# Projection panels moved among the head-norm spreads and ahead of the differential heads, modulation groups and bias copies placed anew, and GpSimd's products taking two tensors

## Chip, cores and metric

The kernel runs on one core of a Trainium2 chip. The metric is the device time of one execution in microseconds, lower is better.

## The reference

Two networks run one after the other, in float32. Block 1 (two layers, 256 tokens and 16 meta tokens, width 1024) does in each layer: an RMS norm; one input projection `h @ w_in` that gives the queries, keys and values of three attentions and 3 x 1024 gate logits; latent attention (8 heads, RMS-normed and rotated q and k); stick-breaking attention (8 heads, a suffix sum of log weights in place of the softmax); differential attention (4 heads, `softmax(q1 k1) - lam * softmax(q2 k2)`, its output normed again); `merged = sum over three branches of sigmoid(gate) * (out @ w_branch)`; an output projection; and a feed-forward with squared ReLU and width 4096. The last layer computes 256 tokens only after the attentions' keys.

Block 2 (two layers, 256 tokens and 256 context tokens) has a SwiGLU of width 2816, a mixer (retention in layer 0, neighbourhood attention in layer 1) and another SwiGLU. Each is entered through a norm with scale and shift and left through a gate. These come from the modulation, which depends on no token:

```
s_c, s_cc = silu(c), silu(c_ctx)
ml, mc = s_c @ w_mod[i] + b_mod[i], s_cc @ w_mod[i] + b_mod[i]     # 9 * 1024 columns each, for i in 0, 1
```

## The kernel before

**Weights.** All large weights come as 632 panels of 128 x 1024 floats. SyncE loads a panel into one of four slots of `raw` as soon as TensorE has finished the panel that was there (L354). ScalarE copies it rounded to float32r (`whi`, L961), VectorE subtracts to get the rest (`wlo`, L1487), and TensorE multiplies three times: high weights by high inputs, high by low, low by high (L454 to L456 for features, L544 to L546 for the token-major values). One panel of features is 24 multiplications; four quarter panels (`token_quarter`) make 512 value columns and hold three PSUM banks until the last. Panels are used strictly in the order in which the host lays them out.

**Order of work.** It is written out by hand, once per engine; the engines meet through semaphore counts, so a step that moves on TensorE must move in ScalarE's and VectorE's programs too. Four PSUM banks (0 to 3) go round for results of panels, banks 4 to 7 serve attention. In each layer of block 1 TensorE does: eight feature panels; the latent up-projections with one panel after each of four of them (`UP_FILL`); `units`, 24 heads of queries and keys, each a sum of squares (L657) and a rotation (L660), with a filler panel after two of every three (`UNIT_FILL`, 14 of 16; fillers 0 to 7 are features, 8 to 15 quarter panels), then the last two fillers (L667) while ScalarE takes roots and VectorE their reciprocal (L1721); `spread`, which brings the inverse roots of each head to all partitions (L676), VectorE rescaling the head right behind it (`normed`, L1729), at most four spreads ahead of it; latent heads, stick heads 0 to 7, differential heads 0 to 3 with 2, 2, 2 and 1 features (`DIFF_FILL`, L815); the branch panels, for each pair `mp` of output chunks and branch `br` in turn; then the output projection and the feed-forward. Branch panels with `br` 2 need `olo`, the low part of the normed differential outputs.

**Gates and exps.** ScalarE evacuates a gate feature with `gate()` (which first waits for its panel) and computes the exps of the next differential head with `diff_exps`, in program order.

**Modulation.** The 144 chunks of 128 outputs of both layers are made in 36 groups of four on GpSimd, beside everything else (L370 to L420). A group works through four panels of `w_mod` with 16 products (a weight panel by one column of `cs`, L384) and 14 sums (L386), strictly in turn, into `macc`, which exists once. Then `mod_group` on TensorE (L474) sums `macc` over the partitions with eight matmuls (L480, recorded as sixteen), after a wait for all of the group's steps, and GpSimd's next group waits for that:

```
pool.wait_ge(mod_done, g)                  # before the first product of group g
...
lane.take(mod_step, MS)                    # TensorE: 30 steps of the group are done
```

The constants in L82 to L84 say after which unit, stick head, differential head, tile or residual chunk TensorE takes a group. Each layer of block 1 has nine: units, end of the spreads, a stick head, a differential head, after branch pair 1, before the feed-forward, after 20 of its tiles, and after chunks m=1 and m=5 of its second product (`residual_tiles`, K=32, four panels for each m). The rest stand in block 2: after 12, 24 and 36 tiles of a SwiGLU's first product, after m=1 and m=5 of its second, and in the retention likewise.

Between group 12 (the one taken in layer 1's differential heads) and group 13 (the one taken at its branch panels) GpSimd issues sixteen copies that write the attention bias table, repeated for every column, to DRAM (L427).

Of the kernel before, what the change touches and what calls it, by code (L numbers as in the profile page):

```python
# [81 lines left out]
MOD_UNIT, MOD_STICK, MOD_DIFF, MOD_BRANCH = (12,), (2,), (1,), (1,)  # L82
MOD_FF, MOD_FF2, MOD_RET, MOD_FF3 = (1, 5), (1, 5), (1, 5), (1,)
# [5 lines left out]
UNIT_FILL = tuple(u for u in range(21) if u % 3)  # L89
UNIT_LAG = 2  # L90
DIFF_FILL = (2, 2, 2, 1)
# [89 lines left out]
def build_program(nc, t):  # L181

    ctx = ExitStack()
    with ctx:
# [181 lines left out]
        def _(pool):  # L366
# [7 lines left out]
            def mod_group(g, last=False):  # L374
# [3 lines left out]
                def step(out, a, b, op):  # L378

                    nonlocal steps  # L380
                    if steps or not (isinstance(g, int) and g == 0):
                        pool.wait_ge(mod_step, g * MS + steps)
                    if op is ALU.mult:
                        pool.tensor_scalar(out, a, b, None, op).then_inc(mod_step, 1)  # L384
                    else:
                        pool.tensor_tensor(out, a, b, op).then_inc(mod_step, 1)  # L386
                    steps += 1

                acc = [macc[:, s * 512:(s + 1) * 512] for s in range(2)]
                for q in range(4):  # L390
                    s = q % 2
                    w = [modraw[:, s * PW + k * 512:s * PW + (k + 1) * 512] for k in range(2)]
                    c = [[cs[:, 4 * q + 2 * k + stream:4 * q + 2 * k + stream + 1] for k in range(2)] for stream in range(2)]
# [54 lines left out]
        def _(pe):  # L448
# [189 lines left out]
            def units():  # L638
# [28 lines left out]
                for n in range(len(UNIT_FILL), 16):  # L667
                    filler(n)
                lane.settle(u_rot)
                lane.take(u_inv)  # L670

# [41 lines left out]
            for layer in range(DEPTH):  # L713
# [10 lines left out]
                units()  # L724

                for j in range(2 * MH):
# [3 lines left out]
                    spread(j, 4 + j % 4)  # L730
                lane.settle(u_out)
                scores(4, qm, km, 0, 0, MQK)
                scores(5, qm, km, T1, 0, MQK)
                for j in range(2 * MH, 24):
                    lane.take(u_out, lag=2)
                    spread(j, 6 + j % 2)
                mod_group()
# [70 lines left out]
                lane.take(arg_ready)  # L808

                for hh in range(DH):  # L810
# [9 lines left out]
                    if hh in MOD_DIFF:  # L820
                        mod_group()
# [21 lines left out]
                lane.take(olo_ready, DH)  # L843
                branch(0, 2)
                for mp in range(1, NC // 2):
                    for br in range(3):
                        branch(mp, br)
                    if mp in MOD_BRANCH:
                        mod_group()
# [102 lines left out]
        def _(act):  # L952
# [98 lines left out]
            for layer in range(DEPTH):  # L1051
# [88 lines left out]
                for n in range(len(UNIT_FILL), 16):  # L1140
                    filler(n)
                lane.tile.add()
# [27 lines left out]
                exps(0, 0)  # L1170
                for hh in range(MH):
# [45 lines left out]
                head_hi(4 + (SH - 1) // 2, 64 * ((SH - 1) % 2))  # L1217

                for hh in range(DH):
# [11 lines left out]
                    lane.tile.add(1 + (hh in MOD_DIFF))  # L1231
# [21 lines left out]
                for mp in range(NC // 2):  # L1253
                    for br in range(3):
                        next_panel()
                        lane.tile.add(2)
                        if br == 0 and mp + 1 < NC // 2:
                            sigmoids(mp + 1)
# [213 lines left out]
        def _(dve):  # L1472
# [169 lines left out]
            for layer in range(DEPTH):  # L1642
# [180 lines left out]
                head_lo(4 + (SH - 1) // 2, 64 * ((SH - 1) % 2))  # L1823

# [4 lines left out]
                for hh in range(DH):  # L1829
# [19 lines left out]
                    if hh - 1 in MOD_DIFF:  # L1849
                        mod_tiles()  # L1850
# [21 lines left out]
                def branch(mp, br):  # L1872
# [23 lines left out]
                    elif mp:  # L1896
# [8 lines left out]
                branch(0, 1)  # L1905
                branch(0, 2)
                for mp in range(1, NC // 2):
                    for br in range(3):
                        branch(mp, br)
                    if mp in MOD_BRANCH:  # L1910
# [344 lines left out]
def all_panels(a):  # L2255

    out = []
    for l in range(DEPTH):
# [9 lines left out]
        out.append(wb.transpose(3, 0, 2, 4, 1, 5).reshape(-1, P, PW))  # L2268
# [79 lines left out]
```

## Time and profile before

| What | Value |
|---|---|
| median of 3 runs | 3621.97 us (3619.17 to 3635.52) |
| the profiled execution | 3621.35 us |
| span of its instructions | 3619.6 us |
| TensorE busy, share of the span | 3306.0 us, 91% |
| VectorE, ScalarE, GpSimd busy | 50%, 36%, 53% |
| mean granted TensorE clock | 0.944 |
| panels, mean traffic | 632 of 512 KB, 119 GB/s |

Times in rows are microseconds from the start of the span, unless marked ns. PE is TensorE's matmul, PEld its weight load, DVE VectorE, ACT ScalarE, POOL GpSimd, SP SyncE. PEclk is the granted share of TensorE's clock of 2.4 GHz, so 0.5 is 1.2 GHz. "Idle before <- X" is the engine's idle time just before the instruction and what ended it. A float32 matmul is recorded as two instructions, so the sixteen of L480 are eight in the code. Matmul ends are modelled and overlap the next start.

### The profile page before, as it was taken

How to read it: one execution, taken by the hardware profiler on the slowest of the kernel's cores; microseconds unless marked ns; L12 is line 12 of the kernel's file. 1: busy time of each engine (PE TensorE's matmuls, PEld its weight loads, DVE VectorE, ACT ScalarE, POOL GpSimd, SP SyncE). 2: the span in 40 equal slices, each digit the busy share in tenths (PEclk: the TensorE clock that was granted, in tenths of full speed). 3: DMA queues.
4: the chain of work that ended last, by engine and by line, in shares of the span. 5: the costliest groups of instructions: out<-in, count | busy, mean ns of one | idle time of the engine just before them, and what ended most of it. 6: DMA issues, size and time to landing. Idle time of an engine off the chain costs nothing.

```text
span 3619.6 us, 49159 instructions
## 1 busy us (share of the span) xinstructions
PE 3306.0 (91%) x18070; PEld 2752.1 (76%) x18070; DVE 1805.0 (50%) x2502; ACT 1292.0 (36%) x2179; POOL 1908.0 (53%) x1277
## 2 busy tenths in 40 slices
PE   7999789899984898899999889989999999998899
PEld 5676689876763898788877757768887888785799
DVE  5665666456543674544352344354435443426554
ACT  3445445343542363322232233232223222235443
POOL 6565878925665788378655003846876565001000
PEclk9989889998987899999999999999999999999999
DMA  4322345532265465233333102323333333331254
GB/s 174 111 82 82 128 146 198 183 124 92 94 122 110 142 212 181 100 122 127 120 119 115 64 0 93 116 99 116 128 122 105 110 122 105 101 111 54 83 184 158
DMA packets 120281, 430.37 MB, mean 119 GB/s; under 512 B 13856, under 2 KB 17184, under 8 KB 119728
## 3 DMA queue, kind: packets, MB, share of 16 engines
q1 hardware_dynamic: 93632, 335.24, 27.5%
q0 software_dynamic: 24576, 86.46, 7.9%
q10 hardware_dynamic: 1904, 6.36, 0.5%
q8 instruction: 113, 1.85, 0.2%
q14 instruction: 56, 0.46, 0.0%
HBM read 426.95 MB, written 8.85 MB: 120 GB/s over the span
## 4 chain that ended last, share of the span: by engine, by line
PE 56%; DVE 5%; POOL 3%; issue 1%; ACT 1%; DMA 0%; DVEq 0%; ACTq 0%; SPq 0%; POOLq 0%
PE ps L454 16%; PE ps L456 15%; PE ps L455 15%; DVE xlo L1542 1%; PE ps L544 1%; PE ps L545 1%; PE ps L546 1%; PE ps L480 1%; POOL macc L386 1%; PE ps L927 1%; DVE tmp L1548 1%; PE ps L882 1%; POOL modraw L384 1%; POOL mprod L384 1%; PE ps L871 1%
## 5 line engine op out<-in xcount | busy, mean ns | idle before, releaser
L1487 DVE TENSOR_TENSOR wlo<-raw,whi 128x1024 fp32r<-128x1024 f32 x632 | 877.7, 1390 | 1087.6 <-ACT whi L961 1064.7
L961 ACT ACTIVATE whi<-raw 128x1024 fp32r<-128x1024 f32 x632 | 668.1, 1058 | 1525.9 <-PE ps L456 1083.9
L454 PE MATMUL ps<-xhi,whi 128*128 128x512 f32 (+2 forms) x3008 | 1033.1, 343 | 48.3 <-DVE xlo L1542 33.1
L456 PE MATMUL ps<-xhi,wlo 128*128 128x512 f32 (+2 forms) x3008 | 1015.5, 338 | 0.0
L455 PE MATMUL ps<-xlo,whi 128*128 128x512 f32 (+2 forms) x3008 | 1015.3, 338 | 0.0
L454 PEld LDWEIGHTS ps<-xhi,whi 128*128 128x128 f32 x3008 | 581.6, 193 | 130.6 <-issue 44.4
L456 PEld LDWEIGHTS ps<-xhi,wlo 128*128 128x128 f32 x3008 | 581.0, 193 | 55.1
L455 PEld LDWEIGHTS ps<-xlo,whi 128*128 128x128 f32 x3008 | 581.9, 193 | 53.9
L384 POOL TENSOR_SCALAR macc<-modraw,cs 128x512 f32<-128x512 f32 x36 | 74.6, 2072 | 949.6 <-PE ps L480 939.0
L384 POOL TENSOR_SCALAR modraw<-modraw,cs 128x512 f32<-128x512 f32 x288 | 526.8, 1829 | 27.6
L384 POOL TENSOR_SCALAR mprod<-modraw,cs 128x512 f32<-128x512 f32 x252 | 447.3, 1775 | 18.9 <-POOL macc L386 0.2
L386 POOL TENSOR_TENSOR macc<-macc,mprod 128x512 f32<-128x512 f32 x252 | 361.4, 1434 | 21.0
L386 POOL TENSOR_TENSOR macc<-macc,modraw 128x512 f32<-128x512 f32 x216 | 327.1, 1514 | 17.5
L454 PE MATMUL ps<-ghi,whi 128*128 128x512 f32 (+1 forms) x704 | 259.0, 368 | 0.0
L455 PE MATMUL ps<-glo,whi 128*128 128x512 f32 (+1 forms) x704 | 258.2, 367 | 0.0
L456 PE MATMUL ps<-ghi,wlo 128*128 128x512 f32 (+1 forms) x704 | 258.2, 367 | 0.0
L443 POOL DMA_DIRECT2D bia<-bias_by_column x32 | 20.9, 658 | 309.0 <-DVE nsc L2141 189.9
L480 PE MATMUL ps<-con,macc 128*128 128x1 f32 x576 | 83.3, 274 | 79.3 <-POOL macc L386 79.3
L456 PEld LDWEIGHTS ps<-ghi,wlo 128*128 128x128 f32 x704 | 132.3, 188 | 24.0
L455 PEld LDWEIGHTS ps<-glo,whi 128*128 128x128 f32 x704 | 132.4, 188 | 23.6
L454 PEld LDWEIGHTS ps<-ghi,whi 128*128 128x128 f32 x704 | 132.4, 188 | 23.6
L454 PE MATMUL ps<-fhi,whi 128*128 128x272 f32 (+1 forms) x512 | 148.3, 290 | 1.5 <-issue 1.5
(339 smaller groups left out, 4782.3 us busy)
## 6 DMA issues: line engine op xcount, KB each, us to landing
raw<-in_panels SPq DMA_DIRECT2D x632, 512.0 KB, 3.3
modraw<-in_mod POOLq DMA_DIRECT2D x144, 512.0 KB, 3.8
bias_by_column<-in_rpb POOLq DMA_DIRECT2D x16, 476.2 KB, 38.4
bia<-bias_by_column POOLq DMA_DIRECT2D x32, 96.0 KB, 2.6
rtab<-in_rtab ACTq DMA_DIRECT2D x2, 1312.0 KB, 9.4
wuq<-in_wuq ACTq DMA_DIRECT2D x2, 768.0 KB, 6.6
con<-in_con SPq DMA_DIRECT2D x1, 1345.5 KB, 12.2
h<-in_x SPq DMA_DIRECT2D x1, 1088.0 KB, 6.8
```

The source lines that it names most:

```text
L384: pool.tensor_scalar(out, a, b, None, op).then_inc(mod_step, 1)
L386: pool.tensor_tensor(out, a, b, op).then_inc(mod_step, 1)
L454: pe.matmul(out, w_hi, x_hi, start=start, stop=False)
L455: pe.matmul(out, w_hi, x_lo, start=False, stop=False)
L456: return pe.matmul(out, w_lo, x_hi, start=False, stop=stop)
L480: last = pe.matmul(bank(b, 2 * j + s, 2 * j + s + 1), macc[:, s * 512 + j * P:s * 512 + (j + 1) * P], ones[:, 0:1], start=True, stop=True)
L544: pe.matmul(out, xh, wh(4 * kk, 512), start=(k == 0), stop=False)
L545: pe.matmul(out, xl, wh(4 * kk, 512), start=False, stop=False)
L546: last = pe.matmul(out, xh, wl(4 * kk, 512), start=False, stop=(k == NC - 1))
L871: last = pe.matmul(bank(4 + i // 2, (i % 2) * 256, (i % 2) * 256 + 256), qk2[:, k + kt * P:k + (kt + 1) * P], qk2[:, q + q0:q + q0 + NX], ...
L961: act.activation(whi[:, s * PW:(s + 1) * PW], raw[:, s * PW:(s + 1) * PW], ACT.Copy).then_inc(hi_split, 1)
L1487: dve.tensor_tensor(wlo[:, s * PW:(s + 1) * PW], raw[:, s * PW:(s + 1) * PW], whi[:, s * PW:(s + 1) * PW].bitcast(F32), ALU.subtract).then ...
```

## The change

Five things change; the arithmetic of the result is the same.

1. GpSimd's products are `tensor_tensor` with the column of `cs` broadcast along 512 elements by a stride of zero. Before they were `tensor_scalar` with the column as a per-partition scalar.
2. Groups are taken after unit 6 in place of 12, after stick heads 0 and 6 in place of stick head 2 and differential head 1, and after m=6 in place of m=5 of the second products. The order of groups against the bias copies stays, so the group ahead of the copies is now the one of stick head 6.
3. The unit loop has a filler after every other unit (11), one filler follows it, and one each stands after spreads 4, 9, 14 and 19.
4. Two features stand ahead of the differential heads, whose own number falls from 2, 2, 2, 1 to 1, 2, 1, 1.
5. Branch panel (1, 0) comes ahead of (0, 2), and the low part of a merged pair is made one panel later.

```diff
-MOD_UNIT, MOD_STICK, MOD_DIFF, MOD_BRANCH = (12,), (2,), (1,), (1,)
-MOD_FF, MOD_FF2, MOD_RET, MOD_FF3 = (1, 5), (1, 5), (1, 5), (1,)
+MOD_UNIT, MOD_STICK, MOD_BRANCH = (6,), (0, 6), (1,)
+MOD_FF, MOD_FF2, MOD_RET, MOD_FF3 = (1, 6), (1, 6), (1, 6), (1,)
-UNIT_FILL = tuple(u for u in range(21) if u % 3)
+UNIT_FILL = tuple(u for u in range(1, 22) if u % 2)
+UNIT_FILLS, SPREAD_FILL = len(UNIT_FILL) + 1, (4, 9, 14, 19)
-DIFF_FILL = (2, 2, 2, 1)
+BRANCH_ORDER = ((0, 0), (0, 1), (1, 0), (0, 2), (1, 1), (1, 2)) + tuple((mp, br) for mp in (2, 3) for br in range(3))
+DIFF_LEAD, DIFF_FILL = 2, (1, 2, 1, 1)
...
 # gpsimd
-                    if op is ALU.mult:
-                        pool.tensor_scalar(out, a, b, None, op).then_inc(mod_step, 1)
-                    else:
-                        pool.tensor_tensor(out, a, b, op).then_inc(mod_step, 1)
+                    pool.tensor_tensor(out, a, b, op).then_inc(mod_step, 1)
...
-                    c = [[cs[:, 4 * q + 2 * k + stream:4 * q + 2 * k + stream + 1] for k in range(2)] for stream in range(2)]
+                    c = [[cs[:, 4 * q + 2 * k + stream:4 * q + 2 * k + stream + 1].broadcast_to([P, 512]) for k in range(2)] for stream in range(2)]
...
 # tensor
-                for n in range(len(UNIT_FILL), 16):
+                for n in range(len(UNIT_FILL), UNIT_FILLS):
                     filler(n)
...
                     spread(j, 4 + j % 4)
+                    if j in SPREAD_FILL:
+                        filler(UNIT_FILLS + SPREAD_FILL.index(j))
...
                 lane.take(arg_ready)
+                for _ in range(DIFF_LEAD):
+                    feature(T)
...
-                lane.take(olo_ready, DH)
-                branch(0, 2)
-                for mp in range(1, NC // 2):
-                    for br in range(3):
-                        branch(mp, br)
-                    if mp in MOD_BRANCH:
+                for mp, br in BRANCH_ORDER[2:]:
+                    if (mp, br) == (0, 2):
+                        lane.take(olo_ready, DH)
+                    branch(mp, br)
+                    if br == 2 and mp in MOD_BRANCH:
                         mod_group()
...
 # scalar
-                for n in range(len(UNIT_FILL), 16):
+                for n in range(len(UNIT_FILL), 15):
                     filler(n)
-                lane.tile.add()
...
                 exps(0, 0)
+                filler(15)
+                lane.tile.add()
...
                 head_hi(4 + (SH - 1) // 2, 64 * ((SH - 1) % 2))
+                lane.tile.add(SH - 1 in MOD_STICK)
+                for _ in range(DIFF_LEAD):
+                    gate()
...
 # vector
                 for j in range(2 * MH):
                     normed(j)
+                    if j == 3:
+                        for n in range(len(UNIT_FILL), UNIT_FILLS):
+                            filler(n)
+                    elif j > 4 and j - 5 in SPREAD_FILL:
+                        filler(UNIT_FILLS + SPREAD_FILL.index(j - 5))
...
                 for j in range(2 * MH + 4, 24):
                     normed(j)
+                    if j == 20:
+                        filler(14)
                 latent_probs(0)
-                for n in range(len(UNIT_FILL), 16):
-                    filler(n)
+                filler(15)
...
-                    for _ in range(DIFF_FILL[hh - 1] if hh else 1):
+                    for _ in range(DIFF_FILL[hh - 1] if hh else 1 + DIFF_LEAD):
...
-                    elif mp:
+                    if br == 1 and mp:
                         merged_lo(mp - 1)
...
 # host
-        out.append(wb.transpose(3, 0, 2, 4, 1, 5).reshape(-1, P, PW))
+        out.append(wb.transpose(3, 0, 2, 4, 1, 5).reshape(-1, P, PW)[[3 * mp + br for mp, br in BRANCH_ORDER]])
```

## Rows read from the trace of the kernel before

**Rows 1.** TensorE's list of waits: who ended them, us in total, times, longest

```profile
PE ps L480 <- POOL macc L386: 79.3, 6, 33.4
...
PE ps L454 <- DVE xlo L1542: 33.1, 25, 3.3
...
PE ps L454 <- DVE olo L1904: 6.3, 2, 3.1
```

**Rows 2.** timeline, TensorE, L480: start us, us, instruction, count, [idle before]

```profile
425.48 3.54 PE L480 MATMUL ps<-con,macc 128*128 128x1 f32 x16 [16.44 <-POOL macc L386]
...
627.66 1.84 PE L480 MATMUL ps<-con,macc 128*128 128x1 f32 x16
...
688.62 3.54 PE L480 MATMUL ps<-con,macc 128*128 128x1 f32 x16 [10.77 <-POOL macc L386]
...
1175.83 3.54 PE L480 MATMUL ps<-con,macc 128*128 128x1 f32 x16 [33.42 <-POOL macc L386]
...
1427.75 3.54 PE L480 MATMUL ps<-con,macc 128*128 128x1 f32 x16 [11.36 <-POOL macc L386]
...
2343.57 3.54 PE L480 MATMUL ps<-con,macc 128*128 128x1 f32 x16 [7.14 <-POOL macc L386]
```

**Rows 3.** timeline, GpSimd, L427: the sixteen bias copies

```profile
1042.45 11.86 POOL L427 DMA_DIRECT2D bias_by_column<-in_rpb  x15
...
1121.00 0.79 POOL L427 DMA_DIRECT2D bias_by_column<-in_rpb  x1 [66.69 <-issue]
```

**Rows 4.** windows: stretch, length, busy us per engine, PEclk, DMA share, GB/s

```profile
88.00:168.00 80.00, 79.63 (x411) 53.61 (x412) 46.02 (x80) 37.01 (x73) 35.51 (x23) 1.00 0.32 106
177.00:215.00 38.00, 37.16 (x139) 24.63 (x138) 20.63 (x56) 6.88 (x23) 16.86 (x13) 0.55 0.09 31
337.00:352.00 15.00, 11.38 (x50) 9.39 (x51) 9.05 (x29) 3.42 (x15) 8.84 (x7) 0.66 0.16 54
425.00:433.00 8.00, 7.52 (x34) 7.55 (x35) 0.17 (x1) 0.00 (x0) 4.63 (x5) 0.51 0.21 66
989.00:996.00 7.00, 7.00 (x24) 4.09 (x24) 2.60 (x6) 2.11 (x5) 6.63 (x5) 0.52 0.01 2
```

**Rows 5.** page, part 5: GpSimd's products (L384) and one kind of sum

```profile
L384 POOL TENSOR_SCALAR macc<-modraw,cs 128x512 f32<-128x512 f32 x36 | 74.6, 2072 | 949.6 <-PE ps L480 939.0
...
L384 POOL TENSOR_SCALAR mprod<-modraw,cs 128x512 f32<-128x512 f32 x252 | 447.3, 1775 | 18.9 <-POOL macc L386 0.2
...
L386 POOL TENSOR_TENSOR macc<-macc,mprod 128x512 f32<-128x512 f32 x252 | 361.4, 1434 | 21.0
```

**Rows 6.** lines L384 and L386: ns min/median/max, first and last start

```profile
L384 POOL TENSOR_SCALAR mprod<-modraw,cs x252: 1564/1575/3473, 14.8 to 3024.6; 128x512 f32<-128x512 f32 x126
...
L386 POOL TENSOR_TENSOR macc<-macc,modraw x216: 1261/1302/2882, 34.9 to 3033.3; 128x512 f32<-128x512 f32 x108
```

**Rows 7.** timeline, TensorE: last products of stick heads 0 and 6, both layers

```profile
273.22 0.38 PE L805 MATMUL ps<-stick_z,vs 128*64 128x128 f32 x2
...
326.50 0.38 PE L805 MATMUL ps<-stick_z,vs 128*64 128x128 f32 x2
...
969.34 0.38 PE L805 MATMUL ps<-stick_z,vs 128*64 128x128 f32 x2
...
1024.57 0.38 PE L805 MATMUL ps<-stick_z,vs 128*64 128x128 f32 x2
```

**Rows 8.** DMA issues between 1040 and 1125 us: KB each, median us to landing

```profile
raw<-in_panels SPq DMA_DIRECT2D x8, 512.0 KB, 20.9
```

**Rows 9.** timeline, TensorE: first of two quarter panels; the first sixteen spreads

```profile
168.80 0.50 PE L544 MATMUL ps<-whi,xhi 128*128 128x512 f32 x1
...
177.34 11.96 PE L676 MATMUL ps<-rs,con 32*96 32x272 f32 x32
```

**Rows 10.** timeline, DVE: the reciprocal of the head norms' roots

```profile
174.73 1.84 DVE L1721 RECIPROCAL rs<-rs 32x272 f32<-32x272 f32 x1
```

**Rows 11.** timeline, TensorE: transposes of differential head 0, layer 0

```profile
340.62 1.35 PE L692 MATMUL ps<-con,att 128*128 128x128 f32 x6 [4.27 <-DVE att L1844]
```

More of the change, by code:

```diff
@@ L88 @@
 UP_FILL = (3, 7, 11, 15)
-UNIT_FILL = tuple(u for u in range(21) if u % 3)
+UNIT_FILL = tuple(u for u in range(1, 22) if u % 2)
+UNIT_FILLS, SPREAD_FILL = len(UNIT_FILL) + 1, (4, 9, 14, 19)
+assert UNIT_FILLS + len(SPREAD_FILL) == 16
 UNIT_LAG = 2
-DIFF_FILL = (2, 2, 2, 1)
+BRANCH_ORDER = ((0, 0), (0, 1), (1, 0), (0, 2), (1, 1), (1, 2)) + tuple((mp, br) for mp in (2, 3) for br in range(3))
+DIFF_LEAD, DIFF_FILL = 2, (1, 2, 1, 1)
 GATE_ORDER = tuple(range(2 * NC, 3 * NC)) + tuple(range(2 * NC))
@@ L670, in units @@
                 lane.take(u_inv)
+                return filler
             def spread(j, b):
@@ L723, in _ @@
                 up()
-                units()
+                filler = units()
                 for j in range(2 * MH):
@@ L736, in _ @@
                     spread(j, 6 + j % 2)
+                    if j in SPREAD_FILL:
+                        filler(UNIT_FILLS + SPREAD_FILL.index(j))
                 mod_group()
@@ L819, in _ @@
                     values(new_bank(), vd, hh * P, P, 0, 1728)
-                    if hh in MOD_DIFF:
-                        mod_group()
                 lane.take(sc_used, 2)
@@ L1230, in _ @@
                     act.activation(dout[:, hh * T1:(hh + 1) * T1], bank(b, 0, T1), ACT.Copy).then_inc(bank_free[b], 1)
-                    lane.tile.add(1 + (hh in MOD_DIFF))
+                    lane.tile.add()
                 lane.take(do_ps)
@@ L1251, in _ @@
                     act.activation(ohi[:, c * T1:(c + 1) * T1], dout[:, hh * T1:(hh + 1) * T1], ACT.Copy).then_inc(ohi_ready, 1)
[L1253 to L1258, printed above, removed]
+                for mp, br in BRANCH_ORDER:
+                    next_panel()
+                    lane.tile.add(2)
+                    if br == 0 and mp + 1 < NC // 2:
+                        sigmoids(mp + 1)
+                    if br < 2:
+                        continue
                     lane.tile.add(mp in MOD_BRANCH)
@@ L1823, in _ @@
                 head_lo(4 + (SH - 1) // 2, 64 * ((SH - 1) % 2))
+                if SH - 1 in MOD_STICK:
+                    mod_tiles()
+                lane.tile.add(DIFF_LEAD)
                 lam_init = 0.8 - 0.6 * math.exp(-0.3 * layer)
@@ L1845, in _ @@
                     last.then_inc(p_ready, 1)
-                    for _ in range(DIFF_FILL[hh - 1] if hh else 1):
+                    for _ in range(DIFF_FILL[hh - 1] if hh else 1 + DIFF_LEAD):
                         lane.panel.add()
                         split()
-                    if hh - 1 in MOD_DIFF:
-                        mod_tiles()
                     lane.tile.add(DIFF_FILL[hh] + 1)
@@ L1904, in _ @@
                     dve.tensor_tensor(olo[:, c * T1:(c + 1) * T1], v, ohi[:, c * T1:(c + 1) * T1].bitcast(F32), ALU.subtract).then_inc(olo_ready, 1)
[L1905 to L1910, printed above, removed]
+                for mp, br in BRANCH_ORDER[1:]:
+                    branch(mp, br)
+                    if br == 2 and mp in MOD_BRANCH:
                         mod_tiles()
```

## The prediction

> **What bounds the kernel now.** I read TensorE's (PE's) list of waits, the timeline at each long wait, what GpSimd (POOL) did before it, and the granted clock by stage. PE is the busiest engine and ends nearly every stage, so time comes only from its stalls and from stretches at half its clock. The largest stall is for modulation: 79.3 us in six waits of L480 for POOL's last sum [rows 1], five of them real: 16.4, 10.8, 33.4, 11.4 and 7.1 us [rows 2]. One POOL group lasts 54.0 us: it starts behind the sixteenth bias copy at 1121.8 and PE gets it at 1175.8 [rows 2, 3]. The 33.4 us is not arithmetic alone: POOL issues fifteen copies at 1042.5, stands 66.7 us, and only then begins the group that PE wants at 1142.4 [rows 3]. The other loss is clock. From 177 to 215 us, where the inverse roots are spread, the granted clock is 0.55 (1.2 GHz most of the time) though PE is counted busy 37.2 of 38 us; around the first differential head it is 0.66, and after the 16.4 us wait 0.51 [rows 4].
>
> **Groups moved, products changed.** A group is 16 products and 14 sums. Products as TENSOR_SCALAR take 1775 ns on average, sums of two tensors 1434 ns [rows 5]. No row has a product with a broadcast second tensor. Bounds: 1.26 us, the shortest two-tensor instruction, and 2.88, the longest [rows 6]; I take 1.47, since size and number of streams are those of the sums. A group gets 16 x 0.3 = 4.8 us shorter: 49.2.
>
> The rows show products at 1575 ns and sums at 1302 ns at the median, the two-tensor form being the quicker [rows 6]. The Trainium skill (GPSIMD Engine Reference, Elementwise — side-by-side cycle accounting) says the opposite: two inputs share one read port, 2.6 cycles an element against 1.8 in the best one-input loop. By that page a product would gain 0.34 us (an estimate from its figures) and the sum below would come out above 3550; the trace's order is against it.
>
> Wait by wait:
> - Layer 0, branch panels, 16.4 us. The group before it leaves the differential heads for stick head 6, over at 326.9 [rows 7]. POOL starts near 329 and ends by 378 (383 at the old price); PE asks at 409.0 [rows 2]. Gone. Its feeder, from stick head 0 (273.6) to 6: 53.3 us less 2 for PE's own modulation products leaves 51 [rows 7], 2 more than 49.2. Late next if the price doesn't fall: 54 against 51.
> - Second feed-forward product of layer 0, m=5 to m=6, 10.8 us. From m=1 (627.7) PE reached m=5 at 677.85 [rows 2], so 12.1 us per m with the group's 1.84 taken off; it will ask at 690, and even the old POOL was ready at 688.5. Gone.
> - The same in layer 1 (256 columns for 272, so 11.4 per m), 11.4 us: PE asks when the old POOL was ready. In the retention residual (2 panels of 512 columns per m, again about 11.4), 7.1 us. Both gone.
> - After a wait PE ran some 7.5 us at half clock (8 us at 0.51 [rows 4]), 3.6 us lost. Four waits gone give 14.5.
> - Layer 1, branch panels, 33.4 us: the group ahead of the bias copies now starts after stick head 0 (969.7, plus 2) and ends at about 1021; the copies start 21 us earlier than at 1042.5. They took 78.6 us [rows 3]; more panels beside them may add 0 to 4, I take 2. The next group ends at 1021.4 + 80.6 + 49.2, about 1151.5, for 1175.8: gain 24 (14 to 31, with products at 1.8 or 1.3). PE gets there sooner than before: in this stretch panels need 20.9 us to land [rows 8] and starve the differential heads, while a stick head uses one panel in 8 to 9 us and hides that. What PE gains there becomes wait for POOL, so nothing else in layer 1 between stick head 6 and the branches counts.
>
> Sum: 16.4 + 10.8 + 11.4 + 7.1 + 24 + 14.5 = 84.2.
>
> **Panels among the spreads.** Two quarter panels took 8.5 us ahead of the spreads (168.8 to 177.3) [rows 9]; one stays there, four now stand after spreads 4, 9, 14 and 19, three come out of the unit loop. PE's work is unchanged. In the unit loop DVE is busy 46 of 80 us at full clock [rows 4], so with thinner filling PE stays the bound. The gain is clock: 0.55 over 38 us [rows 4] is 17 us lost in layer 0, and about 15 in layer 1, which repeats it. Against it: the cover of the root chain shrinks. The last reciprocal starts at 174.7, takes 1.84 and ends 0.8 us before PE needs it [rows 9, 10]; one quarter (4.3 us) less cover and one weight split less ahead of it on DVE leave PE a wait of 1 to 2 us, and a short fall of the clock may remain. I take 13.5 + 12 = 25.5 (8 to 31). ACT's and DVE's splits for these panels stand among the rescalings, which may lag four spreads; a quarter panel of PE work covers them, and without that cover each would cost PE the time of a split.
>
> **Lead of the differential heads.** PE waits 4.27 us for head 0 [rows 11], then runs at 0.66 over 15 us [rows 4]: about 9 us. Two features (6 us, from 12.1 for four panels) ahead of it cover DVE's scaling. But the exps of head 1 now queue on ACT behind two gates, some 7 us later, and the copies of head 0's transposes behind them; heads 0, 2 and 3 have one feature as cover. I keep 7.5 in layer 0 (3 to 9); layer 1's is inside its POOL wait. The branch order puts (1,0) ahead of the wait for olo, 3.1 us in each layer [rows 1]: 3.1 in layer 0, layer 1's hidden likewise. The merged low parts come one panel later, far ahead of their use: nothing.
>
> **Costs.** A group between two stick heads leaves a stretch without a panel; in layer 1 that after head 2 fell to 0.54 for 7 us [rows 4], in layer 0 it didn't. Three such places count now (0 and 6, and 0 in layer 1) for two: -4.5, nearer to the bad case since the scores behind head 6 are longer (+3.5 to -7). POOL reads two streams all the time, and DVE's two-input work feels it; PE waits 33.1 us for the low parts of normed inputs [rows 1], and an eighth more is -4 (0 to -10).
>
> Net: 84.2 + 25.5 + 7.5 + 3.1 - 4.5 - 4 = 111.8. The profiled execution took 3621.35 us (span 3619.6, 1.75 around it), 0.6 below the median of the three runs. 3621.35 - 111.8 = 3509.6; I say 3510.
>
> **Rivals.**
> - The broadcast product costs what the scalar one did. For: the same loop may bind both. It loses 9.6 in layer 1's chain, 3 at stick head 6 and 1.7 of clock: 3524.
> - The products get slower, to the 2072 ns that the first of each group takes [rows 5]: two reads through one port, beside DVE. A group of 58.8. Waits: 7.8 at stick head 6, 19.2 in layer 1 (two groups), 2.3 and 2.3 in the residuals, 10 of clock: 3552. Against it, every sum reads two streams and has a median of 1302 ns. It is the direction that the GPSIMD page of the Trainium skill gives.
> - Slower than before: the stride-zero operand costs a second pass, 2 x 1.43 = 2.9 us, a group of 72. PE then waits at stick head 6 (21), layer 0's m=6 (12), layer 1's branches (2 x 23) and m=6 (15.5), retention (15.5), and at the groups 62 and 61 us apart in the first feed-forward product (20 panels) and from there to m=1 (12 panels and two m), 10 and 11 in each layer, 42; with 14 of clock, 3510 + 166 = 3676. It decides from a product of about 2.6 us, where such waits make up the 112. Only single disturbed sums are that long.
> - The spreads gain nothing: the roots' wait grows, DVE's splits hold up the rescaling, the clock falls again. For: this stretch has the thinnest PE work; against: units with panels between them run at 1.00 [rows 4]. 3535.
> - That the change doesn't do what it says is unlikely: order and weights move together.
>
> **Chances.** Forecast 0.60; price unchanged 0.12; spreads without gain 0.14; slower products 0.08; second pass 0.05; the rest 0.01. A difference of 0.5% (18 us) is about what a measurement of this kernel can tell from none. Faster 0.91, same 0.04, slower 0.05. The forecast's own terms vary together by some 20 (spreads 17 down, 5 up; copies 10 and 7). With 3524, 3535 and 3552 inside, the range is 3486 to 3553.
>
> **What would show it.** Right: L384 as TENSOR_TENSOR near 1.5 us, groups near 49; one wait of PE for POOL, about 35 us, at layer 1's branches; a granted clock near 1.0 from 165 to 205; no 4.27 us gap at head 0. Wrong: products of 1.8 or more, L480 waits at stick head 6, a clock near 0.5 among the spreads, PE waiting over 3 us for the reciprocal.

## The result, and the profile after

The changed kernel took 3591.03 us at the median (3589.59 to 3595.97), the kernel before 3621.97 (3615.06 to 3635.52), five runs each: a ratio of 0.9911, 95% interval 0.9887 to 0.9935. The gain is 31 us, not 112, and 3591 lies 38 us above the top of the range. The runs of before that were shared with the experiments had medians of 3621 to 3627 us in each batch, so the experiments are compared by their ratios as well as by their medians. One of e3's four runs took 8115.93 us and counts as slow, so e3's ratio and its median below are of the other three.

The page of the changed kernel, its span and busy time by engine:

```profile
span 3594.2 us, 49156 instructions
PE 3309.6 (92%) x18070; PEld 2750.5 (77%) x18070; DVE 1987.9 (55%) x2502; ACT 1296.0 (36%) x2179; POOL 1646.8 (46%) x1277
```

The same view of before had DVE at 1805.0 and POOL at 1908.0 us. GpSimd is busy for 261 us less. VectorE is busy for 183 us more, though nothing was given to it. GpSimd's groups of instructions, which answer to [rows 5]:

```profile
L386 POOL TENSOR_TENSOR macc<-macc,mprod 128x512 f32<-128x512 f32 x252 | 388.5, 1542 | 19.8
L386 POOL TENSOR_TENSOR macc<-macc,modraw 128x512 f32<-128x512 f32 x216 | 344.5, 1595 | 16.9
L386 POOL TENSOR_TENSOR mprod<-modraw,cs 128x512 f32<-128x512 f32 x252 | 321.3, 1275 | 13.8
L386 POOL TENSOR_TENSOR macc<-modraw,cs 128x512 f32<-128x512 f32 x36 | 46.8, 1299 | 1187.4 <-PE ps L480 1176.6 <-ACT cs L1046 10.8
```

The products (`mprod`) fell from 1775 ns on average [rows 5] to 1275, below the 1470 I took. The sums rose from 1434 to 1542. TensorE's list of waits, of the changed kernel, against [rows 1] (us in total, times, longest):

```profile
PE ps L454 <- DVE xlo L1551: 47.5, 29, 5.2
PE ps L705 <- ACT att L1231: 31.9, 2, 16.5
PE ps L573 <- DVE sq L1535: 25.7, 14, 8.5
...
PE ps L454 <- DVE wlo L1496: 10.9, 18, 2.6
```

The 79.3 us for GpSimd are gone from the top of the list. What is left of the largest one, 33.4 us [rows 2], is 1.56 us, and the bias copies run from 1006.0 to 1087.1, 81 us, where I had said 80.6 [rows 3]. Timelines of the changed kernel, TensorE and GpSimd:

```profile
1132.20 1.92 PE L480 MATMUL ps<-con,macc 128*128 128x1 f32 x16 [1.56 <-POOL macc L386]
```

```profile
1006.04 11.95 POOL L427 DMA_DIRECT2D bias_by_column<-in_rpb  x15
1086.32 0.80 POOL L427 DMA_DIRECT2D bias_by_column<-in_rpb  x1 [68.33 <-issue]
```

So nearly 78 us of waits for GpSimd went and the kernel gained 31. Longer waits stand for VectorE's low parts: xlo from 33.1 to 47.5 us, the weights' low parts (wlo) from 3.6 us in 2 waits to 10.9 in 18. The second line of the list, 31.9 us in which TensorE stands for ScalarE's copies of the transposes (`att`) in layer 1's differential heads, has two lines of before as its counterpart, 26.6 us together:

```profile
PE ps L704 <- ACT att L1223: 15.1, 1, 15.1
PE ps L704 <- ACT att L1224: 11.5, 1, 11.5
```

The time between stages (read off the timeline by each stage's first matrix product) shows where it was lost, in us:

```
stretch                               before  after   e1     e3
layer 0, head norms to spreads         88.3   78.5   73.3   71.7
layer 0, spreads to stick heads        87.9   97.7   97.4   97.5
layer 0, stick heads to diff. output  117.9  119.9  131.5  115.7
layer 0, to the next norm             112.7   95.5   89.4   79.3
layer 0, feed-forward                 226.8  221.4  213.3  213.8
layer 1, stick heads to diff. output  151.9  153.7  152.7  134.6
layer 1, to the next norm             131.0  103.3  108.2   78.5
swiglu behind layer 1                 390.3  397.2  392.5  384.4
```

The first two rows belong together, since four quarter panels moved from the one to the other: 176.2 us before and 176.2 after. (e1 and e3 are experiments below.)

### The profile page after: what moved, and what is told of

Same layout as the page of the kernel before. It is cut to its first block, busy times and chain, and to the rows that moved or that the text cites. A ratio compares the mean times of both kernels' runs of the same rounds, so it can differ in the third digit from the quotient of the medians.

```text
span 3594.2 us, 49156 instructions
## 1 busy us (share of the span) xinstructions
PE 3309.6 (92%) x18070; PEld 2750.5 (77%) x18070; DVE 1987.9 (55%) x2502; ACT 1296.0 (36%) x2179; POOL 1646.8 (46%) x1277
## 4 chain that ended last, share of the span: by engine, by line
PE 58%; DVE 6%; issue 2%; ACT 1%; DMA 1%; DVEq 0%; ACTq 0%; SPq 0%
PE ps L454 16%; PE ps L455 16%; PE ps L456 16%; DVE xlo L1551 2%; PE ps L544 1%; PE ps L546 1%; PE ps L545 1%; PE ps L480 1%; PE ps L931 1%; DVE tmp L1557 1%; PE ps L886 1%; DVE wlo L1496 1%; DMA raw<-in_panels 1%; PE ps L875 1%; PE ps L902 1%
## 5 line engine op out<-in xcount | busy, mean ns | idle before, releaser
L1496 DVE TENSOR_TENSOR wlo<-raw,whi 128x1024 fp32r<-128x1024 f32 x632 | 942.5, 1492 | 1006.0 <-ACT whi L965 977.3
L454 PE MATMUL ps<-xhi,whi 128*128 128x512 f32 (+2 forms) x3008 | 1041.9, 346 | 69.4 <-DVE xlo L1551 47.5
L386 POOL TENSOR_TENSOR macc<-modraw,cs 128x512 f32<-128x512 f32 x36 | 46.8, 1299 | 1187.4 <-PE ps L480 1176.6
L386 POOL TENSOR_TENSOR macc<-macc,mprod 128x512 f32<-128x512 f32 x252 | 388.5, 1542 | 19.8
L386 POOL TENSOR_TENSOR modraw<-modraw,cs 128x512 f32<-128x512 f32 x288 | 369.8, 1284 | 22.6
L386 POOL TENSOR_TENSOR macc<-macc,modraw 128x512 f32<-128x512 f32 x216 | 344.5, 1595 | 16.9
L386 POOL TENSOR_TENSOR mprod<-modraw,cs 128x512 f32<-128x512 f32 x252 | 321.3, 1275 | 13.8
L443 POOL DMA_DIRECT2D bia<-bias_by_column x32 | 20.9, 657 | 317.4 <-DVE nsc L2154 189.9
L1983 DVE TENSOR_TENSOR sq<-tmp,ps 128x512 f32<-128x512 f32 (+1 forms) x88 | 54.6, 621 | 172.8 <-PE ps L456 172.0
```

Source lines behind the costliest of these rows:

```text
L454: pe.matmul(out, w_hi, x_hi, start=start, stop=False)
L1496: dve.tensor_tensor(wlo[:, s * PW:(s + 1) * PW], raw[:, s * PW:(s + 1) * PW], whi[:, s * PW:(s + 1) * PW].bitcast(F32), ALU.subtract).then ...
L1983: dve.tensor_tensor(w_, v, bank(b, 0, T), ALU.mult).then_inc(bank_free[b], 1)
```

## The experiments

**Theory A:** products with two streams hold up VectorE's operations that read two tensors from SBUF, and that takes back what the rest gains. **Rivals:** the shorter products are good and something else was lost (the panels' new places, a collision of transfers), or the products are harmless and the groups simply lay better before.

### The products' form, alone and taken back

e1 is the changed kernel with scalar products (and the coefficient not broadcast, which the lines below leave out). e2 is the kernel before with the same lines the other way, so that it has products of two tensors. The edit of e1:

```diff
-                    pool.tensor_tensor(out, a, b, op).then_inc(mod_step, 1)
+                    if op is ALU.mult:
+                        pool.tensor_scalar(out, a, b, None, op).then_inc(mod_step, 1)
+                    else:
+                        pool.tensor_tensor(out, a, b, op).then_inc(mod_step, 1)
```

> The changed kernel with GpSimd's products as before (TENSOR_SCALAR); order, groups and panels stay changed. Theory A (the missing gain went to VectorE: products that read two streams block its two-input work, which then holds TensorE): wlo falls from 1492 to under 1400 ns, VectorE's busy time by 100 us or more, a block 2 SwiGLU beside modulation from 397 and 399 to 390 and 391 us; back come some 20 us at layer 1's branches and 3 to 5 at stick head 6 in each layer; together 3545 to 3575 us, below the changed kernel's 3591. Rival B (the missing gain lies in the moved panels and groups themselves): no such gain, and the waits for GpSimd return: 3600 to 3615 us.

> The kernel before with the products alone changed to two tensors. Theory A: groups of about 47 us, four of the five long waits gone and layer 1's down to some 25 us, worth 65 us with the clock behind them, but VectorE slowed by 150 us or more and TensorE held in norms and feed-forward: 3600 to 3625 us, no clear gain. Rival B: the whole 65 us show: 3550 to 3565 us.

Measured: 3556.21 us for e1 (ratio 0.9809, 0.9788 to 0.9830) and 3620.78 for e2 (0.9990, 0.9976 to 1.0004), each in the band of theory A. Taking the new products out of the change makes it 35 us faster; put alone into before they gain nothing, though TensorE's waits for GpSimd fall there from 79.3 to 32.3 us. VectorE's busy time goes with the form both times, on the page of e1 and of e2:

```profile
PE 3302.0 (93%) x18070; PEld 2748.1 (77%) x18070; DVE 1804.9 (51%) x2502; ACT 1293.5 (36%) x2179; POOL 1905.6 (54%) x1277
```

```profile
PE 3332.1 (92%) x18070; PEld 2768.0 (76%) x18070; DVE 1954.3 (54%) x2502; ACT 1293.0 (36%) x2179; POOL 1646.1 (45%) x1277
```

### How much GpSimd does, and what it reads

e3 narrows every operation of GpSimd from 512 to 64 columns (it leaves out seven eighths of the modulation). e4 reads a dense 512-column tensor of constants in place of the broadcast coefficient (its modulation is another one). The lines that matter, without e3's clearing of `macc` and e4's wait for the constants at the start:

```diff
-                    pool.tensor_tensor(out, a, b, op).then_inc(mod_step, 1)
+                    pool.tensor_tensor(out[:, 0:64], a[:, 0:64], b[:, 0:64], op).then_inc(mod_step, 1)
```

```diff
-                    c = [[cs[:, 4 * q + 2 * k + stream:4 * q + 2 * k + stream + 1].broadcast_to([P, 512]) for k in range(2)] for stream in range(2)]
+                    c = [[con[:, 128 * k + 64 * stream:128 * k + 64 * stream + 512] for k in range(2)] for stream in range(2)]
```

> The changed kernel with every product and sum of the modulation over 64 of 512 columns, so the modulation of block 2 is left out for the rest; GpSimd is nearly idle, its DMAs, steps and waits stay. Theory A: no contention and no wait for GpSimd: wlo at 1230 to 1260 ns, 3525 to 3550 us. Rival B: TensorE never waited for more than 2 us for GpSimd in the changed kernel, so 3580 to 3592 us.

> The changed kernel with a 512-wide tile of the constants as the products' second tensor in place of the column repeated by a stride of zero; the modulation is computed with wrong factors. Does the repeated column cost less, for GpSimd or for VectorE? Theory A1 (any second stream does it): products stay at 1.03 us undisturbed, VectorE's busy time and the whole time within 5 us of the changed kernel. Rival A2 (a dense stream is read like the sums'): products at 1.26 us undisturbed, groups some 4 us longer, VectorE slower still: 3595 to 3615 us.

Measured: e3 3446.53 us (0.9520, 0.9489 to 0.9550), 78 us under its band. e4 3648.36 us (1.0068, 1.0038 to 1.0099), slower than before and 33 us above the band of A2. Both misses lie on the side where a higher price of contention would put them. The dose is plain on VectorE: 1556.2 us busy beside narrow groups, 1805 beside scalar products, 1988 beside broadcast ones, 2060 beside dense ones. e3 takes away contention and waits for GpSimd together, so its 145 us below the changed kernel bounds the two and doesn't divide them. It also frees VectorE of the sums, which e1 leaves in.

The same stretch, 88 to 160 us (most of layer 0's unit loop), in windows of after, e1 and e3 (stretch, length, busy us of PE, PEld, DVE, ACT, POOL, then PEclk, DMA share, GB/s):

```profile
88.00:160.00 72.00, 67.29 (x342) 45.96 (x341) 57.67 (x74) 34.12 (x69) 42.92 (x34) 0.95 0.32 106
```

```profile
88.00:160.00 72.00, 71.91 (x371) 48.89 (x371) 52.83 (x85) 34.14 (x68) 49.64 (x32) 0.98 0.30 103
```

```profile
88.00:160.00 72.00, 72.00 (x377) 48.43 (x376) 45.35 (x87) 34.28 (x66) 14.94 (x34) 1.00 0.36 116
```

With the new products TensorE is busy 67.3 us and not 72, and VectorE does 74 instructions in 57.7 us where beside narrow groups it does 87 in 45.4. Which of its instructions? Groups of VectorE's instructions in this window, again after, e1, e3:

```profile
L1496 DVE TENSOR_TENSOR wlo<-raw,whi 128x1024 fp32r<-128x1024 f32 x10 | 17.1, 1708 | 3.0 <-PE ps L456 2.7
L1724 DVE TENSOR_TENSOR km<-km,tmp 96x272 f32<-96x272 f32 x8 | 9.5, 1191 | 0.8
L1720 DVE TENSOR_TENSOR tmp<-ps,con 96x272 f32<-96x272 f32 (+1 forms) x20 | 8.7, 434 | 11.5 <-PE ps L660 11.2
```

```profile
L1499 DVE TENSOR_TENSOR wlo<-raw,whi 128x1024 fp32r<-128x1024 f32 x11 | 13.9, 1259 | 0.4
L1723 DVE TENSOR_TENSOR tmp<-ps,con 96x272 f32<-96x272 f32 (+1 forms) x24 | 10.5, 438 | 17.6 <-PE ps L663 17.2
L1727 DVE TENSOR_TENSOR km<-km,tmp 96x272 f32<-96x272 f32 x8 | 6.8, 852 | 0.8
```

```profile
L1498 DVE TENSOR_TENSOR wlo<-raw,whi 128x1024 fp32r<-128x1024 f32 x12 | 14.7, 1226 | 0.4
L1722 DVE TENSOR_TENSOR tmp<-ps,con 96x272 f32<-96x272 f32 (+1 forms) x23 | 10.1, 438 | 22.9 <-PE ps L662 22.5
L1726 DVE TENSOR_TENSOR km<-km,tmp 96x272 f32<-96x272 f32 x8 | 3.5, 438 | 0.8
```

The instruction on km, both of whose inputs lie in SBUF, takes 438 ns beside narrow groups, 852 beside scalar products with two-tensor sums, and 1191 beside two-tensor products and sums. The one whose first input is in PSUM takes 434 to 438 in all three: it is the control, and it is not touched.

A closer look at single instructions, in e1, in a timeline of VectorE and GpSimd:

```profile
1626.01 1.29 POOL L389 TENSOR_TENSOR macc<-macc,mprod 128x512 f32<-128x512 f32 x1
1626.06 1.78 DVE L1991 TENSOR_TENSOR glo<-sq,ghi 128x512 f32 x1
1627.40 1.88 POOL L387 TENSOR_SCALAR mprod<-modraw,cs 128x512 f32<-128x512 f32 x1
```

glo starts 0.05 us behind a sum and lasts 1.78 us, where one that meets nothing of GpSimd's lasts 0.69: it stood for 1.09 of the sum's 1.29 us. Sorted by what runs beside them, the 512-column glo takes 0.69 us beside a scalar product (all 19 of e1 between 0.68 and 0.70), 1.53 beside a two-tensor product (9 of after), 1.78 beside a sum (e1 and after alike). The instruction on km above takes 0.44 alone, 0.72 on average beside scalar products (11 of e1), 1.34 beside sums. The Trainium skill (SBUF — State Buffer, Who interferes with whom) says that a VectorE instruction with two SBUF inputs contends with a GpSimd instruction that reads SBUF, and that the loser stands for the whole instruction. For GpSimd's two-tensor forms this trace agrees (1.09 of 1.29 us), and the operation with a PSUM input goes untouched, as that page has it for one SBUF input. For its scalar form it doesn't, or only in part: 0.69 us of glo, unchanged, beside an instruction of 1.57.

### The groups, the spreads, the lead

e5 is the kernel before with only the groups moved. e6 and e7 are e1 less one part each: all fillers ahead of the spreads again, or no lead.

```diff
-MOD_UNIT, MOD_STICK, MOD_DIFF, MOD_BRANCH = (12,), (2,), (1,), (1,)
-MOD_FF, MOD_FF2, MOD_RET, MOD_FF3 = (1, 5), (1, 5), (1, 5), (1,)
+MOD_UNIT, MOD_STICK, MOD_DIFF, MOD_BRANCH = (6,), (0, 6), (), (1,)
+MOD_FF, MOD_FF2, MOD_RET, MOD_FF3 = (1, 6), (1, 6), (1, 6), (1,)
```

```diff
-UNIT_FILL = tuple(u for u in range(1, 22) if u % 2)
-UNIT_FILLS, SPREAD_FILL = len(UNIT_FILL) + 1, (4, 9, 14, 19)
+UNIT_FILL = tuple(u for u in range(21) if u % 3)
+UNIT_FILLS, SPREAD_FILL = 16, ()
```

```diff
-DIFF_LEAD, DIFF_FILL = 2, (1, 2, 1, 1)
+DIFF_LEAD, DIFF_FILL = 0, (2, 2, 2, 1)
```

> The kernel before with the modulation groups moved and nothing else (scalar products, old fillers, old order of branches). If the moved groups are what carries the gain of the change (theory A), three of the four waits of TensorE for GpSimd go (16.4, 11.4 and 7.1 us) and the one after the bias copies shrinks little, and the stretches behind them keep the clock: 3565 to 3590 us. If the groups only lay well because panels moved too (rival), 3600 to 3620 us, with waits for GpSimd at the stick heads.

> The kernel after with scalar products (3556 us measured) and the old 16 fillers all ahead of the spreads. Theory A (panels among the spreads are worth little, since VectorE sets the pace there): 4 to 12 us slower than with them, 3560 to 3568 us. Rival (they are worth the 25 us of the prediction and something else took it back): 3575 to 3585 us.

> The kernel after with scalar products (3556 us measured) and no feature panels ahead of the differential heads (fills 2, 2, 2, 1 as before). Theory A (the lead gains nothing: TensorE waits for VectorE in the heads that now have one panel fewer): 3548 to 3560 us. Rival (the lead is worth the 7.5 us of the prediction): 3562 to 3568 us.

Measured, five runs each: e5 3563.70 us (0.9827, 0.9809 to 0.9845), 1 us under its band; e6 3559.54 (0.9822, 0.9800 to 0.9845), e7 3549.09 (0.9790, 0.9772 to 0.9808), in the band of theory A. The moved groups alone give 64 us of e1's 71. The panels among the spreads are worth 3 us by the medians, 5 by the ratios, which these intervals don't tell from nothing; e6 came out just under its band of 3560 to 3568 and far from the rival's 3575 to 3585. Without the lead the kernel is no slower.

Why do the spreads give so little? Timelines of TensorE, e6 in two narrow windows (fifteen of the first spreads, then fourteen of the last), and then e1:

```profile
174.84 3.67 PE L680 MATMUL ps<-rs,con 32*96 32x272 f32 x15
...
179.43 6.55 PE L680 MATMUL ps<-rs,con 32*96 32x272 f32 x14
```

```profile
161.57 2.50 PE L680 MATMUL ps<-rs,con 32*96 32x272 f32 x10
...
183.18 2.56 PE L686 MATMUL ps<-km,qm 96*128 96x128 f32 x16 [0.53 <-DVE km L1741]
...
189.65 0.63 PE L548 MATMUL ps<-whi,xlo 128*128 128x512 f32 x1
190.07 0.63 PE L549 MATMUL ps<-wlo,xhi 128*128 128x512 f32 x1
...
193.27 0.39 PE L548 MATMUL ps<-whi,xlo 128*128 128x512 f32 x1
193.50 0.39 PE L549 MATMUL ps<-wlo,xhi 128*128 128x512 f32 x1
```

The spreads of e6 take 0.24 us each in the first window and 0.47 in the second, with the clock falling from its higher level (2.4 GHz) to its lower (1.2 GHz) between them. So this work does go with the clock. What the panels didn't do is hold the clock. Windows of e6 and of e1:

```profile
176.00:210.00 34.00, 33.16 (x126) 21.66 (x125) 19.61 (x56) 5.83 (x22) 6.97 (x5) 0.55 0.05 16
```

```profile
176.00:210.00 34.00, 32.59 (x157) 21.13 (x156) 17.70 (x48) 8.49 (x26) 8.52 (x6) 0.80 0.15 48
```

In e6 the granted clock is 0.50 from 179 to 209 us. In e1 the panels keep it up to 186 us. Behind the last spreads of the latent heads and the scores, some 7 us without a panel, it is 0.51 from 186 to 193, and the first half of the last quarter panel runs at 0.63 us a product where the rest runs at 0.39. From 200 to 206, behind the last spreads and a modulation group, it is 0.50 again. A difference of 0.25 over 34 us is 8.5 us (an estimate from the two windows), half of the 17 that the prediction put in. From the first rotation of a head norm to the stick heads e1 takes 170.7 us and e6 174.6, and 3.8 us less in layer 1 too. Where the rest of the 8.5 goes stays open; part of it is another fall of the clock, for 3 us in e1's unit loop, where the filling is thinner.

The lead moved a wait. Timelines of TensorE at the transposes, e7 and e1:

```profile
346.36 1.42 PE L696 MATMUL ps<-con,att 128*128 128x128 f32 x6 [4.12 <-DVE att L1865]
```

```profile
358.04 0.88 PE L696 MATMUL ps<-con,att 128*128 128x128 f32 x6 [2.32 <-DVE att L1865]
...
381.81 1.45 PE L696 MATMUL ps<-con,att 128*128 128x128 f32 x6 [2.58 <-DVE att L1865]
```

The 4.1 us at head 0 are gone with the lead; 2.3 and 2.6 us stand at heads 1 and 3, which have one panel each, and 1.6 us more at the products of a head.

The groups at the stick heads have a price of their own. From the stick heads to the differential output layer 0 took 117.9 us before and 131.5 in e1, where the granted clock is 0.53 from 322 to 340 us. e5, with only the groups moved, takes 128.7. The changed kernel takes 119.9 at a clock of 1.00 from 322 to 340, but not for its products alone: e11 below has the same ones and takes 130.1.

### Where the bias copies run

With scalar products TensorE still stood 17.6 us for the group behind the copies. TensorE in e1:

```profile
1122.77 3.55 PE L483 MATMUL ps<-con,macc 128*128 128x1 f32 x16 [17.61 <-POOL macc L389]
```

Nothing reads the copies before the attention at the end. e8 puts all sixteen behind group 24, and e9 puts them in pairs behind eight groups that TensorE takes late. e10 is e9 without the lead. e11 is the changed kernel (two-tensor products) with the pairs. e12 is e10 with two-tensor products in groups 3 and 12 alone. In this order, the edit of e8, the new loop of e9 to e12, and the condition that e12 adds to e1's edit (the coefficient, broadcast in these groups alone, is left out):

```diff
-            for g in range(1, 1 + n_groups // 3):
+            for g in range(1, 1 + 2 * n_groups // 3):
...
-            for g in range(1 + n_groups // 3, n_groups - 1):
+            for g in range(1 + 2 * n_groups // 3, n_groups - 1):
```

```diff
+            made = 0
+            for g in range(1, n_groups):
+                if g - 1 in (0, 1, 4, 9, 18, 22, 23, 27):
+                    for hh in range(made, made + 2):
+                        pool.dma_start(t["skew"][hh, :, :, :],
+                                       t["rpb"][hh, :, :].unsqueeze(1).broadcast_to([15, GW, 127])).then_inc(bias_made, 16)
+                    made += 2
+                if g < n_groups - 1:
+                    mod_group(g)
```

```diff
-                    if op is ALU.mult:
+                    if op is ALU.mult and g not in (3, 12):
```

> The kernel after with scalar products (3556 us measured) and GpSimd's 16 bias copies after group 24, where the next group is due 260 us later, in place of after group 12. Theory A (the wait of 17.6 us at 1122.8 us of that kernel is the rest that the copies cost): 3532 to 3545 us, and group 13 ready some 80 us earlier. Rival (the copies cost as much where they go, through the panels' DMA): 3550 to 3570 us.

> The kernel after with scalar products, and the 16 bias copies in eight pairs, one pair behind each of groups 0, 1, 4, 9, 18, 22, 23 and 27, whose results TensorE takes 24 to 45 us after they are ready. Theory A (each pair costs GpSimd some 10 us of slack and no panel is late): the 27 us that the copies after group 24 gave, and most of the 21 us that they cost in the retrieval stage there: 3505 to 3525 us. Rival (a copy holds the panels up wherever it runs): 3525 to 3545 us.

> The copies in pairs, scalar products, and no feature panels ahead of the differential heads. Theory A (without the lead 7 us faster, as 3549 against 3556 us): 6 to 12 us below the run with the pairs and the lead. Rival (the gain without the lead came through the wait for GpSimd in layer 1, which the pairs take away): within 4 us of it.

> The changed kernel as it is, products of two tensors, with the copies in pairs and nothing else. Theory A (VectorE's slower operations cost 35 us or more beside the scalar products, wherever the copies are; GpSimd's waits are down to 1.6 us there, so the copies cost little): 3575 to 3592 us, VectorE's busy time again 1980 to 1995 us. Rival (the copies cost through the panels' DMA): 3560 to 3572 us.

> As the copies in pairs without the lead, but groups 3 and 12, for which TensorE waited 2 us each, take their products of two tensors. Theory A (5 to 8 us less of GpSimd is worth more there than what VectorE loses, which waits little at the stick heads): 3 to 12 us below the same without. Rival (VectorE's loss is as large here as elsewhere): equal or up to 5 us above.

Measured, five runs each (six of e11):

```
e8   3528.93 us   0.9731 (0.9707 to 0.9755)
e9   3514.18 us   0.9709 (0.9693 to 0.9725)
e10  3523.75 us   0.9715 (0.9697 to 0.9734)
e11  3581.78 us   0.9889 (0.9868 to 0.9911)
e12  3513.93 us   0.9700 (0.9685 to 0.9716)
```

e8 lies 3 us under its band, e9 in it, e11 in it. e8 gains 27 us on e1, and in the retention stage behind group 24 (the expectation calls it retrieval) it loses 21 (542.0 against 521.0 us, by the first matrix product of each stage); e9 takes 517.2 there. So a block of copies costs twice: GpSimd's time, and the stage whose panels share the transfers. In the changed kernel that stage is layer 1's differential heads. TensorE's waits for `att`, 31.9 us there and 30.0 in e1, all but vanish when the block is moved or split; here e8, then e9, then e11:

```profile
PE ps L708 <- ACT att L1234: 3.1, 2, 2.2
```

```profile
PE ps L709 <- ACT att L1235: 0.5, 1, 0.5
```

```profile
PE ps L706 <- ACT att L1232: 3.2, 2, 2.7
```

In program order ScalarE waits for the panels of the gates between these copies to `att`. In the kernel before, a panel took 20.9 us to land beside the copies [rows 8], and in the same stretch of e8 (1040 to 1125 us) 3.3:

```profile
raw<-in_panels SPq DMA_DIRECT2D x20, 512.0 KB, 3.3
```

e9 is 2.9% faster than before and, from the two ratios, 2.0% faster than the changed kernel.

e11 beside e9 is the question of the changed kernel beside e1 again, with most waits for GpSimd gone (9.7 us in e9, 21.8 in e1): two-tensor products cost 68 us there, twice as much as with the copies in a block. The likely reason, which no run shows by itself, is that with the block the shorter group bought back part of its cost where TensorE stood for GpSimd: from layer 1's differential output to the next norm the changed kernel is 5.0 us quicker than e1, but e11 5.8 slower than e9. That is a third of the difference. As much again lies in each of two other stages, layer 0's stick heads to differential output (11.6 quicker against 0.5 slower) and the retention (6.2 quicker against 6.0 slower), and the cause is open there. VectorE on e11's page, 4 us under the 1980 that was expected:

```profile
PE 3313.1 (93%) x18070; PEld 2747.5 (77%) x18070; DVE 1975.8 (55%) x2502; ACT 1293.2 (36%) x2179; POOL 1647.8 (46%) x1277
```

e10 missed theory A: 10 us above e9 by the medians, 2 by the ratios, where 6 to 12 below was expected. With e7 (7 us the other way) the lead's worth is within what these runs can tell from zero. e12's two groups took the waits for GpSimd from 3.3 to 0.7 us; it is 10 us below e10 by the medians, 5 by the ratios, with intervals that overlap, so that theory A is likely there but not settled.

## Why the prediction was wrong

The miss of 81 us has two halves. With the products' old price (-14.3, the first rival) and without the 4 us for contention the prediction would have read 3520 for e1, which took 3556: 36 us. For the products it had a net gain of 10, and the changed kernel stands 35 above e1: 45 us.

- **What failed first** is the last line of the costs: "POOL reads two streams all the time, and DVE's two-input work feels it; PE waits 33.1 us for the low parts of normed inputs, and an eighth more is -4 (0 to -10)". The mechanism was named and mis-sized. I scaled one row of TensorE's waits by an eighth; that row alone rose by 14.4 us, and the cost net of the shorter groups is 35, in e11 against e9 68. VectorE's busy time rises by only a tenth (1804.9 to 1987.9 us), but not evenly: a single instruction doubles or trebles, in stages where VectorE was close behind TensorE, and waits that this brings come with a lower clock (0.95 against 0.98 from 88 to 160 us).
- **Products, 1.47 us.** Right in direction: 1.28 measured, and undisturbed they take 1.04, under my lower bound of 1.26. The shorter group alone is worth nothing net (e2). The rule of the Trainium skill (GPSIMD Engine Reference, Elementwise — side-by-side cycle accounting), two inputs through one port, which I had weighed and set aside, did not make the products slower. The rival built on it, 3552, lay on the right side of the forecast for another reason.
- **Groups and copies, 84.2.** Less the 14.3 that is 70, and 65 with the 4.5 for a group between two stick heads; e5 gave 64. Wait by wait it held, the copies' 81 us too, and from layer 1's stick heads to its next norm the changed kernel gained 26 us, where the prediction had 24 and the clock behind it. That e5's total comes so near is in part luck. The 4.5 was too small (its row reads 0.52, not 0.54): layer 0's stick heads to differential output alone took 11 us more in e5 and 14 in e1. On the other side, layer 1's stick heads to its next norm took 22 us less in e5 (260.6 against 282.9), where the prediction at the old price had 14. And the copies' new place did not free the differential heads from them: they run from 1006 to 1087 us, with the last stick head over at 1027, and TensorE still stands 31.9 us for `att`. The one remaining wait for GpSimd of some 35 us is 17.6 in e1 and 20.2 in e5, and 1.6 in the changed kernel, where TensorE comes later and the group is shorter.
- **Spreads, 25.5.** Measured 3 to 5 by whole runs, 7.7 by the two stages. "0.55 over 38 us [rows 4] is 17 us lost" was right as a loss, since the spreads take 0.24 us at the higher level and 0.47 at the lower. The step that failed is "I take 13.5 + 12", that the panels give nearly all of it back: the clock fell again at 186 us, behind the last spreads of the first sixteen and the scores, and at 200 us, and about half of the loss stayed. This is some 20 of the first half's 36 us. The rival of 3535 named it, "the clock falls again"; its other two reasons, a longer wait for the roots and VectorE's splits, did not show: from the head norms to the stick heads TensorE waits 1.3 us in e1 and 0.8 in e6.
- **Lead, 7.5, and branch order, 3.1.** The lead is worth nothing that can be measured. The text named the exps and copies that queue on ScalarE behind two gates and then kept the gain; TensorE now stands at heads 1 and 3. The branch order was not tried alone: between e5 and e6 it comes together with the lead, for 4 us within the intervals. These are some 10 of the 36. With the spreads' 20 and the groups' 1 or 2 that leaves 4 or 5 us, which the intervals of these runs don't tell from nothing.

## What to carry over

A helper engine's instruction is paid for twice, by its own time and by what it does to the engine that shares its reads: price it by the busy time of the neighbour, with the operations that have both inputs in SBUF counted and those with one in PSUM left out. A shorter form is only worth taking where somebody waits for that engine; elsewhere take the form that disturbs less, even at 1.4 times the duration. A clock loss may be rightly read and still not be yours to take: before it is put in a sum, ask which stretches without a panel the change leaves, since here four panels left about half of it. And a block of transfers is paid for by whoever loads beside it: look for a place where nobody does, or make the blocks small.

## What the runs showed of the hardware

- GpSimd's product of 128 by 512 elements with a broadcast column as second tensor is quicker than a sum of two dense tensors, which I had taken as its floor; with e4's dense second tensor it is not (shortest 1261 ns, as the sums). Rows of the changed kernel, ns min/median/max, product and sum:

```profile
L386 POOL TENSOR_TENSOR mprod<-modraw,cs x252: 1040/1070/3423, 14.5 to 2992.1; 128x512 f32<-128x512 f32 x126
L386 POOL TENSOR_TENSOR macc<-macc,mprod x252: 1261/1354/2376, 16.5 to 2993.5; 128x512 f32<-128x512 f32 x126
```

- The scalar form (1575 ns at the median [rows 6]) is slower on GpSimd and nearly harmless to VectorE (glo 0.69 us alone and beside it, the one on km 0.44 and 0.72); the two-tensor form is faster and harmful (1.53). VectorE's operations with an input in PSUM are untouched by either: all 88 of one line in the changed kernel, 59 of which run beside GpSimd's products or sums, stay between 473 and 483 ns:

```profile
L1557 DVE SCALAR_TENSOR_TENSOR tmp<-h,gsc,ps x88: 473/478/483, 1429.9 to 3396.6; 128x256 f32<-128x256 f32 x88
```

- GpSimd pays too: the same sums take 1542 ns on average in the changed kernel and 1418 in e1, with the same work.
- Beside the block of bias copies a panel takes 20.9 us to land [rows 8], in the same stretch without them 3.3 (e8).
- TensorE's small products go with the clock as large ones do: 0.24 and 0.47 us for a spread, 0.23 and 0.42 from the start of one 512-column product to the next.
